# A two-block transformer on one core: the order of the heads in the dilated attention, and 24 constant products less

## The reference

```python
ATTN_PATTERNS = ((128, 1), (512, 4), (2048, 16))      # window, dilation of a group of heads
HEAD_GROUPS -> 6, 5, 5 heads
...
s = jnp.einsum('bnqrhd,bnkrhd->bnrhqk', qb, kc)
s = jnp.where(mask, s, NEG_INF)
m = jnp.max(s, -1); e = jnp.exp(s - m); den = jnp.sum(e, -1)
o = jnp.einsum('bnrhqk,bnkrhd->bnqrhd', e / den, vc)
lse = m + jnp.log(den)
...
alpha = softmax over the three groups of (logsumexp of the group's lse - log(heads))
merged = concat(o_g * 3 * alpha_g);  y = merged @ w_out
```

## Time and profile before

| | |
|---|---|
| median of 3 runs | 2998.22 us (2997.95 to 3000.17) |
| the profiled execution: time, span of its instructions | 2998.86 us, 2997.2 us |
| busy in the span: TensorE, VectorE, ScalarE | 2951.9, 2155.3, 1270.2 us |
| TensorE's granted clock, mean | 0.996 |
| the steps of the dilated attention, from the first transpose to that of the last step | 630.0 to 677.0 us of the span |

### The profile page before, as it was taken

One profiled execution on the slowest core, in us unless ns is written; L12 is line 12 of the kernel. 1 busy time (PEld: TensorE's weight loads), 2 busy tenths in 40 slices (PEclk: granted clock), 3 DMA queues, 4 the chain that ended last, 5 costly groups with the idle time before them and its releaser, 6 DMA issues.

```text
span 2997.2 us, 46288 instructions
## 1 busy us (share of the span) xinstructions
PE 2951.9 (98%) x17262; PEld 2576.8 (86%) x17262; DVE 2155.3 (72%) x3178; ACT 1270.2 (42%) x1903; POOL 189.1 (6%) x267
## 2 busy tenths in 40 slices
PE   8999999999999999999999999999999999999998
PEld 7888888788888889998887899988998878799987
DVE  7577766665777678775788787867775478788753
ACT  4422323465323245452345555425454244654442
POOL 0000001200000000000130000000000023000000
PEclk9999999999999999999999999999999999999999
DMA  4356563413555533343331133442333332123332
GB/s 150 108 188 198 182 205 116 131 43 99 175 181 191 195 106 102 109 141 116 101 91 63 57 106 105 156 153 85 112 106 102 91 99 86 43 92 100 104 107 76
DMA packets 268315, 357.50 MB, mean 119 GB/s; under 512 B 19906, under 2 KB 211764, under 8 KB 268176
## 3 DMA queue, kind: packets, MB, share of 16 engines
q1 hardware_dynamic: 241344, 270.57, 29.2%
q0 software_dynamic: 26352, 84.74, 8.9%
q10 hardware_dynamic: 480, 0.29, 0.0%
HBM read 348.69 MB, written 2.10 MB: 117 GB/s over the span
## 4 chain that ended last, share of the span: by engine, by line
PE 87%; DVE 9%; ACT 2%; issue 2%; DMA 1%; POOL 0%; DVEq 0%; SPq 0%; ACTq 0%
PE bank L2285 18%; PE bank L2287 18%; PE bank L2286 18%; PE bank L2431 9%; PE bank L2434 9%; PE bank L2433 9%; DVE w_lo L1356 1%; PE bank L2308 1%; PE bank L2311 1%; PE bank L2309 1%; DVE h_f L1412 1%; ACT w_hi L774 1%; DVE h_lo L1418 1%; PE bank L2346 1%; DMA swap<-st 0%
## 5 line engine op out<-in xcount | busy, mean ns | idle before, releaser
L1356 DVE TENSOR_TENSOR w_lo<-raw,w_hi 128x1024 fp32r<-128x1024 f32 x328 | 401.1, 1223 | 493.2 <-ACT w_hi L774 489.6
L774 ACT ACTIVATE w_hi<-raw 128x1024 fp32r<-128x1024 f32 x348 | 368.0, 1058 | 850.6 <-PE bank L2287 806.3
L2285 PE MATMUL bank<-h_hi,w_hi 128*128 128x512 f32 x1376 | 541.7, 394 | 5.3 <-DVE w_lo L1356 3.1
L2287 PE MATMUL bank<-h_hi,w_lo 128*128 128x512 f32 x1376 | 536.2, 390 | 0.0
L2286 PE MATMUL bank<-h_lo,w_hi 128*128 128x512 f32 x1376 | 535.7, 389 | 0.0
L2285 PE MATMUL bank<-act_hi,w_hi 128*128 (+1 forms) x1120 | 437.8, 391 | 0.0
L2287 PE MATMUL bank<-act_hi,w_lo 128*128 (+1 forms) x1120 | 436.1, 389 | 0.0
L2286 PE MATMUL bank<-act_lo,w_hi 128*128 (+1 forms) x1120 | 435.8, 389 | 0.0
L2285 PEld LDWEIGHTS bank<-h_hi,w_hi 128*128 128x128 f32 x1376 | 258.4, 188 | 64.4 <-DVE w_lo L1356 5.5
L2287 PEld LDWEIGHTS bank<-h_hi,w_lo 128*128 128x128 f32 x1376 | 258.3, 188 | 54.6
L2286 PEld LDWEIGHTS bank<-h_lo,w_hi 128*128 128x128 f32 x1376 | 258.5, 188 | 51.9
(11 more groups left out here) (379 smaller groups left out, 5655.2 us busy)
## 6 DMA issues: line engine op xcount, KB each, us to landing
raw<-in_ffn_w_in_dram SPq DMA_DIRECT2D x176, 512.0 KB, 3.5
ada_w<-in_ada_w_dram POOLq DMA_DIRECT2D x72, 1024.0 KB, 5.6
raw<-in_ffn_w_out_dram SPq DMA_DIRECT2D x88, 512.0 KB, 3.8
raw<-in_ffn_w_gate_dram SPq DMA_DIRECT2D x44, 512.0 KB, 3.9
raw<-in_ffn_w_up_dram SPq DMA_DIRECT2D x44, 512.0 KB, 3.9
raw<-in_ffn_w_down_dram SPq DMA_DIRECT2D x44, 512.0 KB, 4.2
raw<-in_mix_w_in_dram SPq DMA_DIRECT2D x44, 512.0 KB, 3.7
raw<-in_attn_w_qkv_dram SPq DMA_DIRECT2D x24, 512.0 KB, 3.7
```

Source lines behind the costliest of these rows:

```text
L774: nc.scalar.activation(w_hi[:, nb % SPL, :], raw_slab(nb), ACT.Copy).then_inc(s_hi, 1)
L1356: V.tensor_tensor(w_lo[:, nb % SPL, :], raw_slab(nb), w_hi[:, nb % SPL, :].bitcast(F32), ALU.subtract).then_inc(s_lo, 1)
L2285: T.matmul(dst, wh, mh, start=first, stop=False)
L2287: return T.matmul(dst, wl, mh, start=False, stop=last)
```

## The change

The pairs of heads are put into another order: a local pair and a strided pair take turns, `(0, 6, 2, 8, 4, 10, 12, 14)` by the first head of each pair. Inside a pair the steps stay as they were. The waits that counted heads by their number now count them by their place in this order. Of the constant products of the steps, the groups at steps 6, 7, 9 and 11 are gone (24 products); those at steps 0, 2 and 3 stay.

```diff
+        PAIRS = (0, 6, 2, 8, 4, 10, 12, 14)
+        ORDER = [h for pair_at in PAIRS for h in (pair_at, pair_at + 1)]
+        PLACE = {h: n for n, h in enumerate(ORDER)}
         A0 = []
-        for pair_at in range(0, HEAD_GROUPS[0][1], 2):
-            for h in (pair_at, pair_at + 1):
-                A0.append((h, 0, [(4 * h, 0, 0, 0, P, 0), (4 * h + 1, P, 0, P, 2 * P, P)]))
-            for h in (pair_at, pair_at + 1):
-                A0.append((h, 3, [(4 * h + 2, 2 * P, P, 0, 2 * P, P), (4 * h + 3, 3 * P, 2 * P, 2 * P, 2 * P, P)]))
-        for g in (1, 2):
-            for h in range(*HEAD_GROUPS[g]):
-                A0.append((h, 0, [(4 * h + r, r * P, r * P, r * P, P, (2 + g) * P) for r in range(4)]))
+        for pair_at in PAIRS:
+            pair_heads = (pair_at, pair_at + 1)
+            if pair_at < HEAD_GROUPS[0][1]:
...
+            else:
+                for h in pair_heads:
+                    g = 1 if h < HEAD_GROUPS[1][1] else 2
+                    A0.append((h, 0, [(4 * h + r, r * P, r * P, r * P, P, (2 + g) * P) for r in range(4)]))
...
-            return sum((g in O_VECTOR) == by_vector for g in range(h + 1))
+            return sum((g in O_VECTOR) == by_vector for g in ORDER[:PLACE[h] + 1])
...
-                    if at == 0 and h >= 2:
-                        act.wait_ge(s_pv, h - 1)
+                    if at == 0 and PLACE[h] >= 2:
+                        act.wait_ge(s_pv, PLACE[h] - 1)
...
-                    act.wait_ge(s_pv, h + 1)
+                    act.wait_ge(s_pv, PLACE[h] + 1)
...
-                    if h >= 2 and h - 2 in O_VECTOR:
-                        pe.wait_ge(s_ov, o_count(h - 2, True))
-                    elif h >= 2:
-                        pe.wait_ge(s_o, o_count(h - 2, False))
+                    before = ORDER[PLACE[h] - 2] if PLACE[h] >= 2 else None
+                    if before in O_VECTOR:
+                        pe.wait_ge(s_ov, o_count(before, True))
+                    elif before is not None:
+                        pe.wait_ge(s_o, o_count(before, False))
...
-                    keep_warm({0: 6, 2: 6, 3: 4, 6: 6, 7: 6, 9: 6, 11: 6}.get(s, 0), 2 + s % 2)
+                    keep_warm({0: 6, 2: 6, 3: 4}.get(s, 0), 2 + s % 2)
```

More of the change, by code:

```diff
@@ L471, in program @@
         ACT0 = {"pool": 0} | {f: 8 + NF * f for f in range(6)}
+        PAIRS = (0, 6, 2, 8, 4, 10, 12, 14)
+        ORDER = [h for pair_at in PAIRS for h in (pair_at, pair_at + 1)]
+        PLACE = {h: n for n, h in enumerate(ORDER)}
         A0 = []
-        for pair_at in range(0, HEAD_GROUPS[0][1], 2):
-            for h in (pair_at, pair_at + 1):
-                A0.append((h, 0, [(4 * h, 0, 0, 0, P, 0), (4 * h + 1, P, 0, P, 2 * P, P)]))
-            for h in (pair_at, pair_at + 1):
-                A0.append((h, 3, [(4 * h + 2, 2 * P, P, 0, 2 * P, P), (4 * h + 3, 3 * P, 2 * P, 2 * P, 2 * P, P)]))
-        for g in (1, 2):
-            for h in range(*HEAD_GROUPS[g]):
-                A0.append((h, 0, [(4 * h + r, r * P, r * P, r * P, P, (2 + g) * P) for r in range(4)]))
+        for pair_at in PAIRS:
+            pair_heads = (pair_at, pair_at + 1)
+            if pair_at < HEAD_GROUPS[0][1]:
+                for h in pair_heads:
+                    A0.append((h, 0, [(4 * h, 0, 0, 0, P, 0), (4 * h + 1, P, 0, P, 2 * P, P)]))
+                for h in pair_heads:
+                    A0.append((h, 3, [(4 * h + 2, 2 * P, P, 0, 2 * P, P), (4 * h + 3, 3 * P, 2 * P, 2 * P, 2 * P, P)]))
+            else:
+                for h in pair_heads:
+                    g = 1 if h < HEAD_GROUPS[1][1] else 2
+                    A0.append((h, 0, [(4 * h + r, r * P, r * P, r * P, P, (2 + g) * P) for r in range(4)]))
         LAST_STEP = {h: s for s, (h, _, _) in enumerate(A0)}
@@ L2101, in o_out @@
                 def o_out(h):
-                    dve.wait_ge(s_pv, h + 1)
+                    dve.wait_ge(s_pv, PLACE[h] + 1)
                     V.tensor_copy(bufs["oT"][0:HD, h // 2, :].rearrange("p (j r) -> p j r", r=4),
```

## The result

| | before | after |
|---|---|---|
| median of 20 runs beside each other | 2998.42 us (2995.92 to 3001.47) | 3004.02 us (3000.03 to 3009.99) |
| ratio after to before | | 1.0018, interval 1.0011 to 1.0025 |
| profiled execution | 2998.86 us | 3000.24 us |
| its span | 2997.2 us | 2998.6 us |
| its mean granted clock | 0.996 | 0.994 |

The changed kernel is 5.6 us slower. That is just under the 0.2% taken as no change, though the interval of the ratio lies wholly above 1. The forecast was 1.2 us faster, and 3004.02 lies outside the range of 2993.5 to 3000.2: the prediction was wrong.

The account below looks back on a forecast made before the run. ScalarE's work plus its 6.6 us of waits was taken to bound the steps. Waits shrinking by 2.0 us less 0.9 given back made 1.2 less: 2998.22 - 1.2 = 2997.0 us, range 2993.5 to 3000.2.

Parts of the forecast that it names:

- The work and the order: In the attention steps, the same work in the new order without the 24 products: 43.8 us against 44.95, 1.2 less.
- The five output waits: ScalarE's waits for output values: heads 0, 2 and 4 together 3.2 us, strided heads 7 and 9 0.6 each.
- The layout: Both orders of the steps laid out, engine by engine with hand-overs: old 44.95 us, new 43.8.
- "about 3": Sign in the profile after: ScalarE's output waits in the steps fall from 4.7 us to about 3.
- The products: Removing the 24 constant products at steps 6, 7, 9 and 11 in the old order: worth 0.4 to 0.5 us.
- The rival that the clock falls: TensorE's clock drops to 1.2 GHz in pauses of the steps: slower, 3004 to 3020 us; chance 0.06.
- +7.5 us for 13 us at half clock: Clock rival's price for one local and one strided pair at half clock: 10.4 us more, pauses covering some 2.9.
- the ring: In the local heads' steps, engines wait for each other in turn; ScalarE idles 4.5 of 19.6 us there.
- The rival's sum: Clock rival's total for one 13 us stretch at half clock: +7.5 us, with the 1.2 taken off +6.3.
- Three waits gone: Rival: output waits of heads 0, 2 and 4 on ScalarE vanish, 4.7 us gained, 2993.5 us; chance 0.13.
- New waits eat the gain: Rival: outputs of heads 7, 9 and 11 each wait 0.9 longer; +2.0 us, 3000.2 us; chance 0.13.
- Nothing arrives: Rival: removed products stood in pauses and waits only change heads; 2998.2 us, give or take 0.5; chance 0.15.

Follow-up runs that it names:

- fifth profile: The changed kernel unchanged, profiled again in a single execution: 2997.70 us, step 0 to step 20 in 44.35 us, no fall of the clock in the steps.
- third profile: The changed kernel unchanged, profiled again in a single execution: 3005.52 us, step 0 to step 20 in 48.99 us, falls behind steps 9 and 15.
- first profile: The changed kernel's original profiled execution: 3000.24 us, step 0 to step 20 in 45.83 us, one fall behind step 9.
- the second and third: Two profiles of the unchanged changed kernel, falls behind steps 9 and 15: 3003.36 us (steps 48.98) and 3005.52 us (steps 48.99).

## Why the prediction was wrong

**The work and the order: right in kind, off in size.** Where the clock holds, the steps take 44.35 us, 0.74 less than before (45.09), where 1.2 less was forecast. The five output waits were where they had been placed: heads 0, 2 and 4 wait 0.96, 0.67 and 1.29 on ScalarE's timeline of the fifth profile, heads 7 and 9 wait 0.56 each. So 4.7 less 2.9 is 1.8 gained (forecast 2.0), and 1.1 given back (forecast 0.9, though 1.2 less 0.4 in its own terms is 0.8). The layout had 0.5 more of waits in the old order than the earlier trace rows show, and 0.4 at strided outputs that show none, so it credited the change with waits that did not exist. The "about 3" named as the sign was also at odds with the prediction's own sum, which left 3.2 and two of 0.6, that is 4.4; measured were 4.1.

**The products: right where the clock holds.** Alone they gave 0.48 in the one profile, as laid out; on the median of their runs no gain shows.

**The clock: the step that failed.** The rival that the clock falls, with a chance of 0.06, is what happens in most profiles. The layout had found one place, a pause of 1.7 us before step 9 (it is 1.61); the one before step 15 (1.18) it did not name. Two arguments then spoke the rival away. The first was the last stretch of the earlier trace rows, busy 16.06 of 19.0 at clock 1.00: it was taken as a share, where the pauses inside matter; the changed kernel's first stretch is busier (17.26 of 19.60), has 0.6 of the 1.61 us of the long pause at its end, and a fall comes 1.8 us behind it. The second was the earlier trace rows: there TensorE's last product ends at 2987.0 and the clock goes to half at about 2990, 3 us later.

```profile
2987.00:2988.00 1.00, 0.01 (x1) 0.00 (x0) 0.92 (x2) 1.00 (x5) 0.00 (x0) 1.00 0.00 0
...
2989.00:2990.00 1.00, 0.00 (x0) 0.00 (x0) 0.77 (x2) 0.76 (x2) 0.00 (x0) 0.98 0.00 0
```

One pause of 3 us at full clock was read as a sign that shorter pauses are safe. In the steps of the changed kernel the clock fell between 0.5 us before the end of the pause of 1.61 us (third profile) and 0.8 us behind it (first). The constant products were priced at the delay that they cause (0.4 to 0.5 us) and not at the clock that they hold. Filling the two pauses, which leaves order and waits alone, takes the changed kernel from 3003.36 in the runs beside it to 2997.03, and the intervals of the two ratios do not overlap (1.0006 to 1.0024, 0.9986 to 1.0004). This shows that the open pauses are the cause, for the steps; what in them the clock answers to is not shown.

The prediction had cited the Trainium skill (TensorE: Matmul & The Clock Gate, section "A second HAM failure mode: psum-queue depth-cycling"), which tells of a kernel that cycles through PSUM banks with short pauses between groups and swings between the two clock levels. The 0.53 and 0.62 behind step 9 and the 0.50 of the third profile agree with the swing. That the cycling of the banks has a part in it no run here shows: the strided stretch before cycles the same banks at 1.00.

**The price of a fall: too high.** The forecast had +7.5 us for 13 us at half clock, 0.58 per us. The first profile's fall is 3.4 us of half clock (of the two stretches of 2 us, twice what the clock lacks of 1.00: 4 x 0.47 + 4 x 0.38); it costs 1.5 (4.23 less 2.72). The two falls of the second and third, some 13.7 us together by the same sum, cost 4.64 (48.99 less 44.35). That is 0.34 to 0.44 per us; it would fit if the waits of the ring take up more than was allowed for, which no run tests. The rival's sum with the 1.2 taken off would have been 3004.5, and measured were 3004.02. That these lie so close is in part luck: the profiles with both falls have only 3.8 to 3.9 more in the steps than before, where the sum has 6.3.

**The rest of the difference.** The median of the changed kernel is 4.4 to 5.6 us above, its profiles with both falls show 3.8 to 3.9 of it in the steps. The mean clock of its runs is 0.0020 lower, which is 0.0020 x 3000 x 2, about 12 us more at half clock in a run: about the two falls. That most runs have both is worked out from this and not seen, since runs without a trace can't be placed; the remaining 0.5 to 1.8 us stay open.

**The other rivals.** Three waits gone: no, 4.1 us are left. New waits eat the gain: 1.1 given back, less than the 1.8 gained. Nothing arrives: 0.74 arrives where the clock holds.

## What to carry to other kernels

Price a filler product by the pause that it stands in, not only by the delay that it causes: before taking it out, lay out the new order and look for TensorE's longest pause, place by place; the busy share of a stretch hides it. A filler issued ahead of the wait, into a free bank, cost nothing here (step 9 came at 18.27 and 18.28 us with and without 11 of them). When one program's profiles differ from each other, take several, and set the mean clock of all runs beside them, as the one profile at hand may be the lucky one.

## What the runs showed of the hardware that was not expected

- The fall does not keep time with the pause. In the first profile TensorE idled until 649.30, and the clock was full until about 650.1 and half until about 653.5, with products running throughout; in the third the clock fell at about 646.3, while TensorE idled until 646.80. Falls of some 3.4 and of some 6.8 us were seen in the steps.
- One and the same program falls in some executions and not in others, with the same pause of 1.61 us (0.53 behind it in the first profile, 1.00 in the fifth).
- A mean clock near 1 hides falls in the kernel before too: with 0.996 over its span it has 0.86 from 1100 to 1125, a stretch in which TensorE is busy all but 0.01 of 25 us by the profile. Busy time hides something there: from 1099.43 to the fall at about 1102.4 TensorE ran products of a single column, behind a pause of 0.84 us. Another fall, at about 1457.4, came behind 24 products of a single column and six constant ones, with a pause of 0.19 ahead of them. So a fall needs no long pause:

```profile
1100.00:1125.00 25.00, 24.99 (x123) 21.96 (x123) 20.72 (x29) 14.82 (x26) 0.00 (x0) 0.86 0.24 72
```

```profile
1099.43 1.05 PE L2359 MATMUL bank<-ones,sumsq 128*128 128x1 f32 x8 [0.84 <-DVE sumsq L1369]
...
1453.86 1.05 PE L2359 MATMUL bank<-ones,sumsq 128*128 128x1 f32 x8 [0.19 <-DVE sumsq L1369]
```

```profile
1456.00:1458.00 2.00, 2.00 (x17) 2.00 (x17) 0.97 (x2) 0.34 (x2) 0.02 (x1) 0.85 1.14 215
1458.00:1460.00 2.00, 2.00 (x9) 1.72 (x8) 1.77 (x4) 0.80 (x2) 0.00 (x0) 0.50 0.83 249
```
